# Weights split into halves in eight slots instead of four, all low halves by VectorE, and the layer norm's rows in another order

## What is computed

```python
for layer in range(DEPTH):                      # DEPTH = 2
    x = x + 0.5 * _swiglu(_rmsnorm(x, ffn_pre_norm[layer]), ffn_pre_w_gu[layer], ffn_pre_w_down[layer])
    h = _rmsnorm(x, mix_norm[layer])
    x = x + (_even_mixer(h, ...) if layer % 2 == 0 else _mla_mixer(h, ...))
    x = x + _memory_cross_attention(_rmsnorm(x, xmem_norm[layer]), _rmsnorm(mem, ...), ...)
    x = x + 0.5 * _swiglu(_rmsnorm(x, ffn_post_norm[layer]), ffn_post_w_gu[layer], ffn_post_w_down[layer])
```

```python
h = layer_norm(DN_ALPHA * h + 0.5 * swiglu(h, ...), ln_g[i, 0], ln_b[i, 0])
h = layer_norm(DN_ALPHA * h + mix, ln_g[i, 1], ln_b[i, 1])
h = layer_norm(DN_ALPHA * h + 0.5 * swiglu(h, ...), ln_g[i, 2], ln_b[i, 2])
h = h + (p[i] @ ple_w_proj[i]) * jax.nn.sigmoid(h @ ple_w_gate[i])
```

## Time and profile before

| | us |
|---|---|
| median of 3 runs | 2406.17 (2405.87 to 2406.98) |
| profiled execution | 2401.76 |
| its span | 2400.0 |
| PE busy | 2275.3 (95%) |
| DVE busy | 1459.4 (61%) |
| ACT busy | 1154.4 (48%) |
| POOL busy | 351.9 (15%) |

### The profile page before, as it was taken

How to read it: one execution, slowest core, us unless ns; L and a number is a source line. 1 busy time by engine, 2 the same in 40 slices (tenths; PEclk the granted TensorE clock), 3 DMA queues, 4 the chain that set the end, 5 groups by cost and what they waited for, 6 DMA issues and landing times.

```text
span 2400.0 us, 26432 instructions
## 1 busy us (share of the span) xinstructions
PE 2275.3 (95%) x10458; PEld 1838.0 (77%) x10458; DVE 1459.4 (61%) x1900; ACT 1154.4 (48%) x1667; POOL 351.9 (15%) x294
## 2 busy tenths in 40 slices
PE   8999988999999989889999999978999999989998
PEld 6887777788788777777887887547887788777886
DVE  6655655555565567555555776876555555576555
ACT  6544555444455457555444443234444444454443
POOL 0002001100100120101003952721001100211001
PEclk9999999999999999999999999989999999999999
DMA  7656433455565552335656665215655666425553
GB/s 262 196 183 208 137 122 118 157 185 184 179 213 181 166 181 84 119 120 178 189 181 196 188 184 172 82 50 184 186 185 163 189 185 187 153 88 185 184 184 122
DMA packets 111148, 396.59 MB, mean 165 GB/s; under 512 B 13232, under 2 KB 14000, under 8 KB 110896
## 3 DMA queue, kind: packets, MB, share of 16 engines
q1 hardware_dynamic: 111024, 394.90, 52.0%
HBM read 393.80 MB, written 1.05 MB: 165 GB/s over the span
## 4 chain that ended last, share of the span: by engine, by line
PE 81%; DVE 11%; POOL 4%; ACT 3%; issue 1%; DMA 1%; SPq 0%; POOLq 0%; DVEq 0%; ACTq 0%
PE bank L548 25%; PE bank L550 24%; PE bank L549 24%; POOL wlo L2559 3%; PE bank L607 2%; DVE wlo L1697 2%; PE bank L596 1%; ACT whi L1116 1%; DVE X L1850 1%; DVE X L1853 1%; PE bank L665 1%; PE bank L651 1%; PE bank L889 0%; PE bank L640 0%; DMA raw<-in_w_x_kv 0%
## 5 line engine op out<-in xcount | busy, mean ns | idle before, releaser
L1697 DVE TENSOR_TENSOR wlo<-raw,whi 128x1024 fp32r<-128x1024 f32 (+2 forms) x659 | 824.2, 1254 | 529.4 <-ACT whi L1116 522.4
L1116 ACT ACTIVATE whi<-raw 128x1024 fp32r<-128x1024 f32 (+2 forms) x718 | 754.7, 1054 | 562.6 <-PE bank L550 556.6
L548 PE MATMUL bank<-whi,XH 128*128 128x512 f32 (+2 forms) x1840 | 733.9, 399 | 22.3 <-DVE root L1794 8.5
L550 PE MATMUL bank<-whi,XL 128*128 128x512 f32 (+2 forms) x1840 | 717.9, 390 | 0.0
L549 PE MATMUL bank<-wlo,XH 128*128 128x512 f32 (+2 forms) x1840 | 717.1, 390 | 0.0
L548 PEld LDWEIGHTS bank<-whi,XH 128*128 128x128 f32 x1840 | 349.7, 190 | 105.6 <-issue 17.4
L2559 POOL TENSOR_TENSOR wlo<-raw,whi 128x1024 fp32r<-128x1024 f32 x59 | 150.6, 2580 | 1845.8 <-ACT whi L1116 1845.8
L550 PEld LDWEIGHTS bank<-whi,XL 128*128 128x128 f32 x1840 | 348.9, 190 | 72.9
L549 PEld LDWEIGHTS bank<-wlo,XH 128*128 128x128 f32 x1840 | 350.0, 190 | 65.9
L548 PE MATMUL bank<-whi,HH 128*128 128x512 f32 x704 | 279.4, 397 | 0.0
L549 PE MATMUL bank<-wlo,HH 128*128 128x512 f32 x704 | 277.6, 394 | 0.0
(11 more groups left out here) (410 smaller groups left out, 2197.4 us busy)
## 6 DMA issues: line engine op xcount, KB each, us to landing
raw<-in_w_w SPq DMA_DIRECT2D x264, 512.0 KB, 3.6
raw<-in_w_gu_pre SPq DMA_DIRECT2D x88, 512.0 KB, 3.8
raw<-in_w_gu_post SPq DMA_DIRECT2D x88, 512.0 KB, 3.6
raw<-in_w_dn_pre SPq DMA_DIRECT2D x44, 512.0 KB, 3.5
raw<-in_w_dn_post SPq DMA_DIRECT2D x44, 512.0 KB, 3.5
raw<-in_w_x_kv SPq DMA_DIRECT2D x32, 512.0 KB, 3.6
raw<-in_w_sbg_in SPq DMA_DIRECT2D x20, 512.0 KB, 3.7
raw<-in_w_x_q SPq DMA_DIRECT2D x16, 512.0 KB, 3.7
```

Of the source, the lines that this page charges most:

```text
L548: pe.e.matmul(o, xh, hi[:, k, :], start=kt == 0, stop=False)
L550: m = pe.e.matmul(o, xl, hi[:, k, :], start=False, stop=kt == kts - 1)
L1116: act.e.activation(whi[v % SPLIT][:, 0:n], raw[v % RAW][:, 0:n], ACT.Copy).then_inc(*hi_ok.did(v))
L1697: dve.e.tensor_tensor(wlo[v % SPLIT][:, 0:n], raw[v % RAW][:, 0:n], whi[v % SPLIT][:, 0:n].bitcast(F32), ALU.subtract).then_inc(*lo_ok.did(v))
```

## The change

Eight slots are held instead of four (`SLOTS = 8`), and the low half is written over the raw unit: `wlo` and `raw` are the same memory. So SP may load unit v when PE has used unit v-8 for the last time; ACT waits for nothing but the load; DVE makes every low half, and POOL none. The splits of the four units after a tail are yielded before the tail's passes (`GROUP = 4` ahead). In the layer norm, statistics and variance of a tile are made as before, the reciprocal comes after the first subtraction, and tile 1's row (`dve_ln_row(key, 1)`) is put off: it is done by DVE at "one 1" of the next stage, ahead of the low halves of tile 1's transposes. Five rows of gains lie in memory that other tiles (`junk`, `sbmask`) use at other times.

```diff
@@ schedule
-        alone = 0 if first else len(mine) - min(SPLIT, len(mine)) if last else len(mine)
+        alone = 0 if first else len(mine) - min(GROUP, len(mine)) if last else len(mine)
             for i, k0, nk in rest:
-                yield "split", i, 0, False
+                yield "split", i, 0
+            if last:
+                yield "split", rest[-1][0], GROUP
                 yield "unit", c, i, k0, nk, 1
-                if not (last and j == len(rest) - 1):
-                    yield "split", i, SPLIT, last
+                if not last:
+                    yield "split", i, GROUP
             if last:
                 yield "flush", (0,)
-                yield "split", rest[-1][0], SPLIT, True
                 yield "out", c, (1,)
@@ memory
-        raw = [sb(f"raw{i}", [128, UNIT]) for i in range(RAW)]
-        whi = [sb(f"whi{i}", [128, UNIT], F32R) for i in range(SPLIT)]
-        wlo = [sb(f"wlo{i}", [128, UNIT], F32R) for i in range(SPLIT)]
+        with ExitStack() as same_place:
+            raw = [sb(f"raw{i}", [128, UNIT], F32, same_place) for i in range(SLOTS)]
+        wlo = [sb(f"wlo{i}", [128, UNIT], F32R) for i in range(SLOTS)]
+        whi = [sb(f"whi{i}", [128, UNIT], F32R) for i in range(SLOTS)]
@@ pe_unit
-                pe.wait_ge(pool_lo_ok if on_pool[u] else lo_ok, u)
+                pe.wait_ge(lo_ok, u)
@@ act_settle
-                act.wait_ge(raw_in[v % RAW], v)
-                if v >= SPLIT:
-                    act.wait_ge(pe_ok, ("used", v - SPLIT))
-                act.e.activation(whi[v % SPLIT][:, 0:n], raw[v % RAW][:, 0:n], ACT.Copy).then_inc(*hi_ok.did(v))
+                act.wait_ge(raw_in[v % SLOTS], v)
+                act.e.activation(whi[v % SLOTS][:, 0:n], raw[v % SLOTS][:, 0:n], ACT.Copy).then_inc(*hi_ok.did(v))
@@ act_ab (dve_ab has the same)
-            for i in (6, 7):
-                act_settle()
-                act_split_to(index["ab_out", i])
+            act_settle()
+            act_split_to(index["ab_out", 7] + GROUP)
@@ dve_mixed
                     if c == 1:
-                        dve_ln_row(key, t)
+                        dve.wait_ge(dve_ok, ("bn", key, 1, t))
+                        dve.e.bn_aggr(mv[:, t, :], bn[:, t, :, :].rearrange("p c n -> p (c n)")).then_inc(*dve_ok.did(("mean", key, t)))
+                        dve.wait_ge(dve_ok, ("mean", key, t))
+                        dve.e.tensor_scalar(mv[:, t, 1:2], mv[:, t, 1:2], 1.0, 1e-5 / ALPHA ** 2, ALU.mult,
+                                            ALU.add).then_inc(*dve_ok.did(("var", "ln", key, t)))
+                        if t == 0:
+                            dve_ln_row(key, 0)
+        def dve_pieces_ln(key):
+
+            return lambda c, tiles: [(1, ("row", key, 1))] * (c == 1 and 1 in tiles) + pieces_ln(key)(c, tiles)
@@ dve_ln_row
-            dve.wait_ge(dve_ok, ("bn", key, 1, t))
-            dve.e.bn_aggr(mv[:, t, :], bn[:, t, :, :].rearrange("p c n -> p (c n)")).then_inc(*dve_ok.did(("mean", key, t)))
-            dve.wait_ge(dve_ok, ("mean", key, t))
-            dve_var(mv[:, t, 1:2], 1.0, 1e-5 / ALPHA ** 2, ("ln", key, t))
             for c in range(2):
+                dve.wait_ge(dve_ok, ("mean", key, t))
                 dve.e.scalar_tensor_tensor(out=xs, in0=xs, scalar=mv[:, t, 0:1], in1=gain(i)[:, cols], op0=ALU.subtract,
                                            op1=ALU.mult).then_inc(*dve_ok.did(("xg", key, c, t)))
-                dve.wait_ge(dve_ok, ("xg", key, c, t))
+                if c == 0:
+                    dve.wait_ge(act_ok, ("sqrt", "ln", key, t))
+                    dve.e.reciprocal(mv[:, t, 1:2], mv[:, t, 1:2]).then_inc(*dve_ok.did(("rstd", "ln", key, t)))
+                dve.wait_ge(dve_ok, ("xg", key, c, t), ("rstd", "ln", key, t))
@@ sp_program
-            for v in range(RAW, len(stream)):
-                for job in points.get(v - RAW, ()):
+            for v in range(4, len(stream)):
+                for job in points.get(v - 4, ()):
                     sp_work(*job)
-                sp.wait_ge(pool_lo_ok if on_pool[v - RAW] else lo_ok, v - RAW)
+                if v >= SLOTS:
+                    sp.wait_ge(pe_ok, ("used", v - SLOTS))
                 sp_load(v)
```

More of the change, by code:

```diff
@@ L321, in hidden_tiles, with row @@
                     sb(f"sg{n}", [128, 2, 2, 256], F32, s), sb(f"hb{n}", [128, 2, 2, 256], F32, s))
-        def row(name, src, s):
+        def row(name, src, s, place=None):
             n = src.shape[0]
-            row_of[name] = sb("row_" + name, [128, n], F32, s)[:, :], src
+            row_of[name] = sb("row_" + name, [128, n], F32, s)[:, :] if place is None else place, src
             row_in[name] = signal("row_in_" + name, 16)
@@ L526, in pe_split @@
                 stream.append((S, 128 * sum(u[2] * u[3] for u in us[:i]), us[i][2] * us[i][3]))
-            while pe_next[0] <= index[S, i] + ahead:
-                on_pool[pe_next[0]] = by_pool
-                pe_next[0] += 1
         def halves_of(u, nk, w):
-            return [x[u % SPLIT][:, 0:nk * w].rearrange("p (k w) -> p k w", k=nk) for x in (whi, wlo)]
+            return [x[u % SLOTS][:, 0:nk * w].rearrange("p (k w) -> p k w", k=nk) for x in (whi, wlo)]
         def pe_unit(S, c, i, k0, nk, tile, lhs, bs):
@@ L981, in pe_ab @@
             for i in (6, 7):
[L982 removed]
+                pe_split("ab_out", i, 0)
             for t in range(2):
@@ L1696, in dve_settle, with dve_split_to @@
                 dve.wait_ge(hi_ok, v)
-                dve.e.tensor_tensor(wlo[v % SPLIT][:, 0:n], raw[v % RAW][:, 0:n], whi[v % SPLIT][:, 0:n].bitcast(F32),
+                dve.e.tensor_tensor(wlo[v % SLOTS][:, 0:n], raw[v % SLOTS][:, 0:n], whi[v % SLOTS][:, 0:n].bitcast(F32),
                                     ALU.subtract).then_inc(*lo_ok.did(v))
-        def dve_split_to(last, by_pool=False):
+        def dve_split_to(last):
             while dve_next[0] <= min(last, len(stream) - 1):
-                if not by_pool:
-                    dve_owed.append(dve_next[0])
+                dve_owed.append(dve_next[0])
                 dve_next[0] += 1
@@ L2432, in dve_ds @@
                 pass
-            for _ in dve_run("c_out", dve_mixed("c_out", "ln11", 1.0), pieces_ln("ln11"), tail=True):
+            for _ in dve_run("c_out", dve_mixed("c_out", "ln11", 1.0), dve_pieces_ln("ln11"), tail=True):
                 pass
@@ L2547, in dve_program @@
             dve_last(1)
-        pool_next = [0]
-        def pool_split_to(last, by_pool=False):
-            while pool_next[0] <= min(last, len(stream) - 1):
-                v = pool_next[0]
-                n = stream[v][2]
-                if by_pool:
-                    pool.wait_ge(hi_ok, v)
-                    pool.e.tensor_tensor(wlo[v % SPLIT][:, 0:n], raw[v % RAW][:, 0:n], whi[v % SPLIT][:, 0:n].bitcast(F32),
-                                         ALU.subtract).then_inc(*pool_lo_ok.did(v))
-                pool_next[0] += 1
         def pool_run(S, out=None, tail=False, hold=False, late=1):
             for what, *a in schedule(S, tail, hold, late):
-                if what == "split":
-                    pool_split_to(index[S, a[0]] + a[1], a[2])
-                elif what == "out" and out:
+                if what == "out" and out:
                     out(*a)
@@ L2863, in sp_load @@
             name, off, n = stream[v]
-            sp.e.dma_start(raw[v % RAW][:, 0:n], d["w_" + name][off:off + 128 * n].rearrange("(p w) -> p w", p=128)).then_inc(
-                *raw_in[v % RAW].did(v))
+            sp.e.dma_start(raw[v % SLOTS][:, 0:n], d["w_" + name][off:off + 128 * n].rearrange("(p w) -> p w", p=128)).then_inc(
+                *raw_in[v % SLOTS].did(v))
         def sp_program():
```

81 lines of the change are left out of this document (27 added, 54 removed).

## The result

The kernel after takes 2339.3 us at the median (2335.1 to 2339.9), the kernel before 2406.1 (2405.9 to 2407.0): a ratio of 0.9724 with a 95% interval of 0.9711 to 0.9738. That median is over four executions, of which one took 3772.6 us at a mean granted clock of 0.556 and is left out of the range and the ratio; the other three have a median of 2338.7. It is 66.8 us faster, where the prediction had 50 and a range that ends at 2344.

What follows compares the result with a forecast made beforehand. PE was taken as the bound, busy 2275.3 of 2400.0 us, so only the other 125 could go. Norm tails 25.1, other tails with ple_g0 20.7 and middle 4.1 sum to 49.9 us off: 2356 us, range 2344 to 2373.

Steps and rivals of the forecast that it cites:

- the norm tails: Six stage ends with a layer norm: 25.1 us off; T1 is the end of tile 1's pass there on PE.
- c_out: Norm tail ln11: close loads land late, so tile 0's first half comes 1.45 us late; gain 1.4 us smaller.
- ab_out: Norm tail ln01: three splits now come first and one stretch of low clock is kept; gain 2.5 us.
- the middle of stages: Between tails: splits wait only for the load, so VectorE's low-half waits at 288 and around 857 go, 4.1 us.
- rival B: Run-ahead gains more: ScalarE and VectorE leave PE's pace in the two mixer stages; 2349 down to 2341 us; chance 0.11.
- the tails without a norm: Stage ends without a layer norm: waits for GpSimd's halves (11.9 us) and line 1771 (5.9) go, less new 0.25 us waits.
- 11.9 us, all gone: Tails without a layer norm: 8.5 us under root L1794 plus 3.4 of GpSimd's low halves vanish, halves being ready before T0.
- 5.9 gone: Four tails with line 1771: waits of 1.5 us each vanish because eight slots let VectorE's splits finish long before.
- ple_g0: Stage whose 4.1 us wait for L2462, from splits before it and GpSimd beside it, goes; 3.9 with the new wait off.
- Rival D: Slower: each load waits for its slot's unit to leave PE; 2416 us if a landing takes 8 us; chance 0.03.
- C: VectorE late in tails, fourth split 1.5 us later in each, middle gives nothing: 2377 us (2366 to 2385); chance 0.17.
- E: GpSimd was never what PE waited for and stalls only change names: 2400 to 2410 us; chance 0.03.

Runs made afterwards that it cites:

- dvehalves: The kernel before with VectorE making the 59 low halves that GpSimd made, at the same places, with four slots: 2373.1 us.
- late: The kernel after with each tail's four splits put back to their old places, one behind each unit of tile 1's pass: 2352.8 us.
- poolearly: The kernel after, but GpSimd makes the low halves of the four units split ahead of each tail, at their new early place: 2340.8 us.
- pace: The kernel after, but ScalarE waits before a high half until PE has used the unit four earlier, splits ahead of tails exempt: 2365.0 us.
- oldrow: The kernel after with the layer norm's rows in the old order: reciprocal before the first multiplication, tile 1's row ahead of the fence: 2335.2 us.
- gainlater: The kernel after with the two gain loads for the norm behind ln02 moved twelve units later in SyncE's queue: 2332.1 us.

## Why the prediction fell short

**Right: the norm tails (25.1, measured 24.6).** Step by step: rows of 0.75 us, no wait for tile 0, 1.01 us for tile 1 (1.05), 7.95 us from T1 to the pass (8.0), no low clock in ln00, ln02, ln10, ln11, ln12. c_out has 2.2 us of waits where 1.45 + 1.05 were expected. ab_out gained 1.8, forecast 2.5, and varies by a microsecond or two with its low clock from run to run. That the stretched rows were GpSimd's doing is shown by dvehalves; that this alone does not free the norm tails, by the new wait for XL there and in late. poolearly adds that with eight slots and early splits the norm tails stay short while GpSimd still makes halves, ln11 but for 0.8.

The Trainium skill, "SBUF — State Buffer", who interferes with whom, has a two-input VectorE instruction and a GpSimd one that reads SBUF shut each other out for a whole instruction. The trace of poolearly agrees, with 2052 ns against a median of 689. What it costs depends on the place: nothing in the tails without a norm, 2.8 us in ple_g0.

**Wrong, the middle of stages (4.1, measured 12.0).** The step that failed: "I put their 4.1 on this part", their being the waits for low halves alone, while the waits for xm_kT and XL L2108 were left for rival B. What that paragraph opens with, "Nothing waits for PE before a split any more, only for the load", was right, and its effect is not only that a low half comes earlier. ScalarE's wait for a slot was in front of everything queued behind it, exponentials and table loads too, and those were on PE's path. The row to read was ScalarE's own, [6.48 <-PE bank L550] at 277.55, a wait of the engine that feeds the late one; the prediction counted PE's waits alone. pace puts that wait back, and with it 13.6 us return in these places. Rival B named the mechanism and got a chance of 0.11 with the argument that "the chain runs through table loads that stay". They stay, but they start earlier. Its upper end of 11.5 us was of the right size; taken as the likeliest value it moves the forecast to 2349.

**Wrong in size: the tails without a norm (16.8, measured 26.0).** The mechanism was right: PE waits for nothing in these twelve tails after. The step that failed is the price, "11.9 us, all gone" and "5.9 gone", waits taken at the idle time in their rows. The term was 1.5 us of idle time in the rows each, while the tails shortened by 2.3 to 2.4 where GpSimd was and by 1.9 elsewhere. A timeline of PE in the kernel before shows the difference:

```profile
206.33 0.39 PE L549 MATMUL bank<-wlo,XH 128*128 128x512 f32 x1
206.56 0.39 PE L550 MATMUL bank<-whi,XL 128*128 128x512 f32 x1
207.08 0.50 PE L548 MATMUL bank<-whi,XH 128*128 128x512 f32 x1
207.42 0.40 PE L549 MATMUL bank<-wlo,XH 128*128 128x512 f32 x1
...
208.35 0.39 PE L550 MATMUL bank<-whi,XL 128*128 128x512 f32 x1
209.95 0.47 PE L548 MATMUL bank<-whi,XH 128*128 128x512 f32 x1 [1.21 <-DVE root L1794]
210.25 0.40 PE L549 MATMUL bank<-wlo,XH 128*128 128x512 f32 x1
```

Matmuls that overlap start 0.23 us apart though one takes 0.39. The row before a wait is counted to its end, so an idle time of 1.21 is a step of 1.60, 1.37 more than 0.23, and the next step is 0.07 to 0.11 longer too. Short stalls vanish almost wholly: the one at 206.56 has 0.13 of idle time, carries no releaser, and costs 0.29 + 0.11. Summed over this tail the steps are 2.1 us too long before where the rows name 1.54 of idle time (0.13, 1.21 and 0.19 for the half at 212.20). Each of the three stalls so cost 0.2 us more than its row says, and the one stall of a tail with line 1771 0.4 more (idle 1.47, gain 1.86).

The four tails with line 1771 were forecast to gain by the slots, which let splits stop waiting for PE; pace shows that this wait is ScalarE's, for with it back all 7.5 us are lost though the slots and the early loads stay. The expected new waits of 0.25 us did not appear.

**Wrong: ple_g0 (3.9, measured 0.2).** The step that failed: "The norm gains in other places: same jobs, same order on SyncE's queue; the jobs now stand before loads that PE frees later anyway." In ple_g0 they do not: PE frees slots in short steps there, and the job's own condition, the end of the row behind the fence, is what moved. The cover was named and not looked at in the one stage where it is missing. The two causes that the prediction gave for the old wait did go (dvehalves, with the old order, gains 3.2 there), and a new wait of the same size took their place. Rival D priced late landings at 7.3 us as far from any row; behind this block they were 6.3 to 7.2.

**The range.** The two errors that make the time shorter (7.9 and 9.2 us) were both biases of method, reading PE's named waits only, and they point the same way; the range covered neither in full. The 3.7 us between profiled executions and medians point that way too and are no matter of mechanism; without them the time would still lie 1 us below the range. That ple_g0's 3.7 went the other way is luck. C, D and E did not happen.

**How the parts add up.** In medians: GpSimd out of the tails 31 (dvehalves against before), ScalarE off PE's pace 25.7 (pace), the splits ahead of the tail 13.5 (late), the order of the rows -4.1 (oldrow): 66.1 of 66.8 us. The agreement to 0.7 is luck: pace and late were measured with the other parts in place and dvehalves without, and by the ratios the four are 30.5, 27.2, 15.4 and -2.9, together 70 of 66.

**Open.** Why the granted clock drops in one execution of the same instructions and not in the next (below), and so how much of the -1.6 in c_in and the swings in ab_out belongs to the change.

## What to carry to other kernels

Before removing a buffer wait, read what is queued behind it on the waiting engine and follow that to the bound engine: here a 6.5 us wait of ScalarE is in no row of PE's waits, which name VectorE at the end of the chain, and 7.7 us went with it at that place. Price a stall of a pipelined engine by the step from start to start, not by the idle time in its row. A DMA queue that is served in order makes every job with a condition a gate for the loads behind it; when the condition moves, check the gate in each stage where it stands, and put a job that nobody needs soon behind the loads.

## What the runs showed of the hardware

The stretches of lower clock in these traces do not always stand in the same places. At 320 to 355 the kernel after has 2.02 us of idle time and no low stretch, and gainlater, with the same instructions and 2.02 us of idle time there, has one of 3.4 us and takes 36.8 instead of 35.2. At 970 to 995, with 2.64 us of idle time each time, before and after have one, oldrow and late none (25.0 against 23.5 us). Such a stretch is worth 1.5 to 1.6 us of the span here, so a difference of that size at one place is no effect of an edit unless the idle time differs as well.

GpSimd's subtraction of 128x1024 takes 2.47 to 2.58 us and VectorE's 1.25. Made ahead of the tails, GpSimd's slower halves cost nothing in the tails without a norm; in ple_g0, beside the sum that PE waited for, they stretched a sum of 0.69 us to 2.72 and cost 2.8.
